# Differential attention in blocks of one query tile, with its value projection by head pair and its head norm taken in three batches

## The reference

```python
def diff_blocks(q, k, v, lam):
    scale = q.shape[-1] ** -0.5
    def blk(qb):
        s = jnp.einsum('bqhsd,bkhsd->bhsqk', qb, k).astype(jnp.float32) * scale
        p = jax.nn.softmax(s, axis=-1)
        a = (p[:, :, 0] - lam * p[:, :, 1]).astype(v.dtype)
        return jnp.einsum('bhqk,bkhd->bqhd', a, v)
    return over_query_blocks(blk, q)
...
    o_diff = diff_blocks(dq, k_d.reshape(b, -1, DIFF_HEADS, 2, DIFF_HD), v_d, lam)
    o_diff = (rmsnorm(o_diff, lp['diff_subln']) * (1.0 - lam_init)).reshape(b, n, GROUP_W)
```

## Time and profile before

| | |
|---|---|
| median of three runs | 2740.01 us (2735.83 to 2743.49) |
| the profiled execution, time | 2737.1 us |
| its span in the trace | 2734.9 us |
| mean granted PE clock | 0.942 |
| busy: PE, DVE, ACT, POOL | 2426.1, 1319.2, 943.0, 172.8 us |

### The profile page before, as it was taken

One profiled execution on the slowest core, in us unless ns is written; L12 is line 12 of the kernel. 1 busy time (PEld: TensorE's weight loads), 2 busy tenths in 40 slices (PEclk: granted clock), 3 DMA queues, 4 the chain that ended last, 5 costly groups with the idle time before them and its releaser, 6 DMA issues. The chain is left out here.

```text
span 2734.9 us, 33688 instructions
## 1 busy us (share of the span) xinstructions
PE 2426.1 (89%) x13152; PEld 1596.1 (58%) x13152; DVE 1319.2 (48%) x2658; ACT 943.0 (34%) x1886; POOL 172.8 (6%) x184
## 2 busy tenths in 40 slices
PE   3999999899898987879859999999988989888798
PEld 1765765674476756554327567557745667565543
DVE  3352664564364474661133426545553644746611
ACT  2242113541253364651022421135412533646510
POOL 0120000001000000001202200010010000000012
PEclk8999999999999998989969999999999989989799
DMA  6430100100100000102155101000001000001021
GB/s 216 165 140 26 50 16 1 48 1 13 58 7 9 3 1 2 63 1 91 60 178 213 61 26 50 16 21 29 1 13 64 1 9 3 1 2 63 1 93 61
DMA packets 72136, 128.42 MB, mean 47 GB/s; under 512 B 22915, under 2 KB 36099, under 8 KB 70341
## 3 DMA queue, kind: packets, MB, share of 16 engines
q1 hardware_dynamic: 71864, 121.52, 13.0%
q10 hardware_dynamic: 112, 4.72, 0.5%
HBM read 109.02 MB, written 21.92 MB: 48 GB/s over the span
## 5 line engine op out<-in xcount | busy, mean ns | idle before, releaser
L609 PE MATMUL psum<-arena 128*32 128x256 f32 (+8 forms) x8496 | 1743.0, 451 | 123.8 <-DMA arena<-in_hy_decay 46.9
L609 PEld LDWEIGHTS psum<-arena 128*32 128x32 f32 (+3 forms) x8496 | 1013.1, 161 | 780.7 <-issue 526.3
L613 PE MATMUL psum<-ident,arena 128*128 128x128 f32 (+1 forms) x2248 | 366.6, 291 | 76.2 <-ACT arena L1284 30.0
L1763 DVE TENSOR_REDUCE st<-psum 128x1 f32<-128x1152 f32 (+1 forms) x288 | 352.0, 1235 | 137.1 <-PE psum L609 135.5
L1469 DVE TENSOR_TENSOR arena<-arena 128x64 f32<-128x64 f32 (+10 forms) x686 | 304.5, 490 | 175.8 <-ACT arena L1420 57.5
L613 PEld LDWEIGHTS psum<-ident,arena 128*128 128x128 f32 (+1 forms) x2248 | 268.1, 146 | 178.6 <-issue 59.7
L1268 ACT ACTIVATE arena<-psum,st 128x1152 f32<-128x1152 f32 (+1 forms) x288 | 324.8, 1129 | 118.8 <-DVE st L1763 115.3
L609 PE MATMUL psum<-k_parts,q_parts 96*128 96x384 f32 (+2 forms) x1000 | 300.4, 391 | 34.4 <-ACT arena L1268 22.9
L1284 ACT COPY arena<-psum 128x512 f32<-128x512 f32 (+1 forms) x344 | 170.6, 505 | 230.3 <-PE psum L613 229.2
L1469 DVE TENSOR_TENSOR arena<-psum,arena 128x512 f32<-128x512 f32 (+2 forms) x136 | 75.1, 553 | 355.6 <-PE psum L609 308.2
L609 PEld LDWEIGHTS psum<-k_parts,q_parts 96*128 96x128 f32 (+1 forms) x1000 | 181.5, 205 | 53.3 <-ACT arena L1268 36.6
(11 more groups left out here) (125 smaller groups left out, 1170.1 us busy)
## 6 DMA issues: line engine op xcount, KB each, us to landing
arena<-in_ada_w SPq DMA_DIRECT2D x12, 2048.0 KB, 9.0
arena<-in_w_in SPq DMA_DIRECT2D x10, 2048.0 KB, 9.0
arena<-out_xs SPq DMA_DIRECT2D x36, 512.0 KB, 4.7
out_xs<-arena SPq DMA_DIRECT2D x18, 512.0 KB, 2.6
arena<-in_w_out SPq DMA_DIRECT2D x4, 2048.0 KB, 7.9
out_xs<-in_x ACTq DMA_DIRECT2D x1, 4608.0 KB, 17.3
spectrum_kept<-arena SPq DMA_DIRECT2D x2, 2304.0 KB, 8.4
arena<-spectrum_kept SPq DMA_DIRECT2D x2, 2304.0 KB, 8.8
```

The lines of the kernel that those rows point to most:

```text
L609: return nc.tensor.matmul(out, lhsT, rhs, start=start, stop=stop)
L613: return nc.tensor.transpose(out, src, ident[0:n, 0:n])
L1763: nc.vector.tensor_reduce(st[:, 16 + x % 4:17 + x % 4], psum[:, 512 * b0:512 * (b0 + nk)].rearrange("p (c n) -> p c n", c=nk)[:, :, 0:w], ...
```

## The change

Differential groups leave `attention` and get programs of their own on PE, ACT and DVE (`diff_attention`). A block becomes one query tile with both heads: nine blocks, and still 18 units and 24 steps. Value products come at every second step from step 4, 36 matmuls of 128 moving columns instead of 256. The output is not divided by the softmax sums: since the head norm divides by the root of the mean square, the sums cancel except in the small constant, which is multiplied by the squared sums instead (`squares`, and four extra matmuls in `head_squares`). So `inverse_sums`, `spread_sums`, `spread_out` and `finish` fall away, and DVE only copies the block out of bank 7 (`read_out`, 128 columns). The norm runs for three batches of blocks, 0 to 3, 4 to 7 and 8, at steps 10, 18 and 20. The value projection for the sample is made in each group for its own two heads, 128 columns wide, in steps 0 to 3 (`sample_values`), and read out in two copies of four tiles. All three gate parts are multiplied before the attention. Banks 6 and 7 alternate by another rule, and four probability buffers replace three. The rotary table (`ROPE_DIFF`) lies elsewhere and is loaded in each group. `VALUE_FILL` is the table of steps 0 to 3.

```diff
-BLOCKS = {g: [(tiles, p) for tiles in QUERY_TILES for p in range(len(PAIRS[g]))] for g in PAIRS}
+QUERY_TILES = {1: [(0, 1), (2, 3), (4, 5), (6, 7), (NT,)], 2: [(t,) for t in range(TT)]}
+BLOCKS = {g: [(tiles, p) for tiles in QUERY_TILES[MAPS[g]] for p in range(len(PAIRS[g]))] for g in PAIRS}
+HEADS_NORMED = ((0, 4), (4, 8), (8, 9))
...
-    if fills(grp, u + 2):
-        return 6
+        return (7, 6, 7)[j] if u % 2 else (6, 6, 7)[j]
...
+        return 2 * (n % 2) + i
...
-def fills(grp, g):
-
-    if grp == "diff0" and g < 5:
-        return [("v", t) for t in ((0, 1), (2, 3), (4, 5), (6,), (7,))[g]]
-    if grp == "diff0":
-        return {7: [("gate", 1, slice(0, 2))], 8: [("gate", 1, slice(2, 5))], 9: [("gate", 1, slice(5, KD))],
-                13: [("gate", 2, slice(0, KD))]}.get(g, [])
-    if grp == "diff1":
-        return {0: [("gate", 1, slice(0, 3))], 1: [("gate", 1, slice(3, 6))], 2: [("gate", 1, slice(6, KD))],
-                4: [("gate", 2, slice(0, KD))]}.get(g, [])
-    return []
+def normed(g):
+
+    return [b for b, (n0, n1) in enumerate(HEADS_NORMED) if g == 2 * (n1 - 1) + 4]
...
-                load(at(ROPE_DIFF, NT, 64), I["rope"][:, :, 0:64], "diff_params")
...
+                    load(at(ROPE_DIFF, NT, 64), I["rope"][:, :, 0:64], "diff_rope", part)
...
+                def sample_values(grp, half, first):
+
+                    job, c = ("v", grp, half), P * int(grp[4])
+                    ps = claim(job, [7]) if first == 0 else bank[7]
+                    for i in (first, first + 1):
+                        t = 4 * half + i
+                        for k in range(KD):
+                            last = mm(ps[:, i * P:(i + 1) * P], hT[:, k, t * P:(t + 1) * P],
+                                      W[:, SLOT["diff_vg", 0], k, c:c + P], k == 0, k == KD - 1)
+                    if first == 2:
+                        last.then_inc(*K.done(job))
...
+                def diff_attention(grp):
+
+
+                    units, steps = UNITS[grp], tail_step(grp)
...
+                    def scores(u, s):
+
+                        n, i, _ = units[u]
+                        t, x = BLOCKS[grp][n][0][0], 2 * u + s
+                        if x >= 2:
+                            pe.wait_ge(*S.at("exps", (grp, x - 2)))
+                        for j, (c, w) in enumerate(chunks(t)):
+                            last = mm(bank[3 * (x % 2) + j][:, 0:w], q_parts[0:96, 2 * i + s, t * P:(t + 1) * P],
+                                      k_parts[0:96, 2 * i + s, c:c + w])
+                        last.then_inc(*S.up("scores", (grp, x)))
+
+                    def turn(u, j):
+
+                        if not (0 <= u < len(units) and j < pieces(grp, u)):
+                            return
+                        number, b = piece_number(grp, u, j), turn_bank(grp, u, j)
+                        pe.wait_ge(*S.at("mixed", (grp, u)))
+                        kts = key_tiles(grp, units[u][0])[4 * j:4 * j + 4]
+                        take_bank(b, S.at("turned_scalar", (grp, number)))
+                        for a in range(len(kts)):
+                            last = flip(bank[b][:, a * P:(a + 1) * P], at(PROB[grp] + (u % 4) * 1152 + (4 * j + a) * P, P))
+                        last.then_inc(*S.up("turned", (grp, number)))
+
+                    def values(n):
+
+                        kts = key_tiles(grp, n)
+                        take_bank(7, S.at("read_out", (grp, n)))
+                        if n == 0:
+                            pe.wait_ge(*K.emptied(("v", "diff", NT)))
+                            pe.wait_ge(*K.emptied(("v", grp, 1)))
+                        pe.wait_ge(*S.at("turned_scalar", (grp, piece_number(grp, 2 * n + 1, pieces(grp, 2 * n + 1) - 1))))
+                        for kt in kts:
+                            for i in range(2):
+                                prob = at(SLOTS[grp], 4, TT, P)[:, slot(grp, 2 * n + i), kts.index(kt), :]
+                                for w in range(2):
+                                    row0, vc = 64 * i + 32 * w, P * int(grp[4]) + 64 * i + 32 * w
+                                    last = mm(bank[7][row0:row0 + 32, 0:P], at(VV + kt * GW + vc, 32), prob,
+                                              kt == kts[0], kt == kts[-1])
+                        last.then_inc(*S.up("values", (grp, n)))
+
+                    def head_squares(b):
+
+                        n0, n1 = HEADS_NORMED[b]
+                        pe.wait_ge(*S.at("head_squares", (grp, b)))
+                        take_bank(7, S.at("roots_begun", (grp, b)))
+                        mm(bank[7][:, 0:(n1 - n0) * P], halves[:, :], at(DQ, (n1 - n0) * P), True, False)
+                        for k in range(n1 - n0):
+                            last = mm(bank[7][:, k * P:(k + 1) * P], at(TH["diff"] + k * P, P), ident[:, :],
+                                      False, k == n1 - n0 - 1)
+                        last.then_inc(*S.up("squares_summed", (grp, b)))
+
...
+                    for g in range(steps):
+                        if g < len(units):
+                            scores(g, 0)
+                        if g % 2:
+                            turn(g - 3, 1)
+                        if g < len(units):
+                            scores(g, 1)
+                        if g in VALUE_FILL:
+                            half, first = VALUE_FILL[g]
+                            if first == 0:
+                                take_bank(7, K.emptied(("v", grp, half)))
+                            sample_values(grp, half, first)
+                        for b in normed(g - 1):
+                            head_squares(b)
+                        turn(g - 3, 2)
+                        if g % 2:
+                            turn(g - 2, 1)
+                        turn(g - 2, 0)
+                        for n in due(grp, g):
+                            values(n)
...
-                        gate("diff", "diff_vg", GW, int(grp[4]), 0, K.next())
+                        for i in range(3):
+                            gate("diff", "diff_vg", GW, int(grp[4]), i, K.next())
...
+                    def head_roots(b):
+
+                        nq = P * (HEADS_NORMED[b][1] - HEADS_NORMED[b][0])
+                        act.wait_ge(*S.at("squares_summed", (grp, b)))
+                        nc.scalar.activation(at(DQ, nq), bank[7][:, 0:nq], ACT.Ln, scale=1.0 / 64
+                                             ).then_inc(*S.up("roots_begun", (grp, b)))
+                        act.wait_ge(*S.at("roots_begun", (grp, b)))
+                        nc.scalar.activation(at(DQ, nq), at(DQ, nq), ACT.Exp, scale=-0.5).then_inc(*S.up("head_roots", (grp, b)))
+
+                    def keep_samples(half):
+
+                        job, c = ("v", grp, half), P * int(grp[4])
+                        act.wait_ge(*K.full(job))
+                        nc.scalar.copy(at(VV, NKEY, GW)[:, 4 * half:4 * half + 4, c:c + P],
+                                       B(job).rearrange("p (a n) -> p a n", a=4)).then_inc(*K.drained(job))
...
+                        take(g - 3, 0)
+                        take(g - 3, 1)
+                        if g % 2 == 0:
+                            take(g - 3, 2)
                         if g < len(units):
                             exps(g, 0)
...
+                        if g == 3:
+                            keep_samples(1)
+                        for b in normed(g - 1):
+                            head_roots(b)
+                        if g % 2:
+                            take(g - 3, 2)
+                        if g < len(units):
+                            exps(g, 1)
+                        if g == 1:
+                            keep_samples(0)
...
+                    def read_out(n):
+
+                        v.wait_ge(*S.at("values", (grp, n)))
+                        nc.vector.tensor_copy(at(DD + n % 4 * P, P), bank[7][:, 0:P]).then_inc(*S.up("read_out", (grp, n)))
+
+                    def squares(b):
+
+                        n0, n1 = HEADS_NORMED[b]
+                        nu, c, d = 2 * (n1 - n0), 24 + 2 * n0 % 16, at(DD, (n1 - n0) * P)
+                        s0 = st[:, c:c + nu].unsqueeze(2).to_broadcast([P, nu, 64])
+                        nc.vector.scalar_tensor_tensor(at(TH["diff"], nu, 64), s0, 64 * EPS, s0, ALU.mult, ALU.mult)
+                        v.wait_ge(*S.at("read_out", (grp, n1 - 1)))
+                        tt(at(DQ, (n1 - n0) * P), d, d, ALU.mult).then_inc(*S.up("head_squares", (grp, b)))
+
+                    def head_norm(b):
+
+                        n0, n1 = HEADS_NORMED[b]
+                        nq = (n1 - n0) * P
+                        out = oT[:, OUT_TILE[grp], n0 * P:n1 * P]
+                        v.wait_ge(*S.at("head_roots", (grp, b)))
+                        link(tt(at(DD, nq), at(DD, nq), at(DQ, nq), ALU.mult))
```

(22 more changed lines are left out.)

295 lines of the change are left out of this document (133 added, 162 removed).

## The result

The changed kernel takes 2667.93 us (median of four runs, 2663.98 to 2677.52) against 2740.6 for the kernel before in the same comparison: a ratio of 0.9742, with a 95% interval of 0.9710 to 0.9773. That is 72.7 us less. The forecast was 2671 us.

The account below looks back on a forecast made before the run. Waits between engines, plus PE's fill in diff0, were taken to bound the differential stages. Body 85.1, tail 17.1 and 8.3 ahead made 110.5 us a stage, 67.2 us gained in two layers: 2671 us, forecast 2655 to 2690, range 2640 to 2708.

Parts of the forecast that it names:

- The pair of units: Two steps of the new pipeline: DVE longest at 8.8 us, slacks 0 to 0.4; 9.4 us taken, against 12.2 before.
- The term for the clock: In the bodies: granted clock stays near 0.85, so a pair takes 9.4 us instead of 8.8.
- the rival with the high clock: Clock stays high and slacks hold: 8.8 us a pair, 15.5 for the tail, 2650 us; chance 0.17.
- The first four units: Start of a body, steps with value projection: 4.9 us of PE each, 22.8 us until the fifth unit's maxima.
- The norm: Blocks 0 to 3, in steps 10 to 12: 3.5 us once a stage, where 1.7 to 1.9 came per block.
- A body: First scores into the last mix: first units, six pairs, norm and ends sum to 85.1 us.
- The tail's sum: Stage end after the last large mix: 15.5 us at full clock, 17.1 with a tail's clock; values 2.0.
- What moves ahead: Before the first scores: two gate parts add 8.3 us per stage; rotary table load hidden, 3 us at most otherwise.
- the signs named ahead: Expected profile: maxima 9.0 to 9.8 us apart, bursts 2.0 to 2.3, bodies 82 to 88, tails 15.5 to 18, clock near 0.85.
- Narrow products bound by issue: Rival in 32 value bursts: 0.082 us a record, 5.9 instead of 2.0 us a burst, 2783 us; chance 0.05.
- The chain: Rival: the chain between engines binds the pairs, not DVE; 10.5 to 11 us a pair, 2702 us; chance 0.15.
- No change in the steps: Rival: the pair stays at 12.2 us, 67 us more over 24 pairs, 2738 us; chance 0.03.

Follow-up runs that it names:

- e13: The changed kernel with every block's value products done twice in place; 2727.04 us, ratio 0.9937.
- e6: The changed kernel with the rotary table of diff0 loaded first among that stage's transfers; 2665.85 us, ratio 0.9742.
- e4: The changed kernel without the small DVE product that multiplies the reciprocal by lambda and the first sum; 2664.57 us, ratio 0.9724.
- e10: The changed kernel with ACT instead of DVE copying a block's output out of bank 7, all but each batch's last block; 2664.61 us, ratio 0.9741.
- e11: The changed kernel with each block's output normed by itself instead of in batches, the norm's place kept; 2700.74 us, ratio 0.9849.
- e12: The changed kernel with each block normed by itself and the norm moved to its old place, ahead of the scores; 2717.83 us, ratio 0.9909.
- e7: The kernel before with all gate parts ahead and one-tile blocks in the differential groups, old order and norm; 2756.31 us, ratio 1.0060.
- e1: The changed kernel with value products over one key tile instead of nine; 2686.74 us, ratio 0.9803.

## Why the prediction was right

**The pair of units** was the main term. DVE was named as the longest at 8.8 us with a slack of 0 to 0.4, and I chose 9.4 for the clock. Measured: 8.89 us, without idle time on DVE. The hand-made schedule held to 0.1 us, and e13 showed its slack behind the values to be as small as worked out (10.7 us expected and measured).

**The term for the clock was mis-sized.** "PE has as much work per time in the new pairs as in diff1 before" was wrong. PE is busy for 69.5 of 81.7 us in diff1's body, 85%, before 73.9 of 98.6, 75%, and the clock there is 0.97, not 0.85. Of the bodies of layer 0, some 15 and 29 us were at 1.2 GHz before, and 4 and 4 are in the change. Six pairs at 0.5 less make 3.1 us a body. So the pairs went as the rival with the high clock has them, not as the forecast; its tail did not.

**The first four units** were put at 22.8 us behind 0.9 of scores; from the first scores (947.38) to the fifth unit's maxima (970.18) are 22.8 in all. Projection steps took 3.73 us (3.6 expected), and the wait of step 3 is the 3.11 in front of 970.18. **The norm** of blocks 0 to 3 was put at 3.5; the four units around it take 21.4 instead of 17.8 us, 3.7 more. **A body** came to 81.8 instead of 85.1.

**The tail's sum left out a burst.** It had one value burst behind the last large unit; there are two, since block 6 comes due in the step after that mix (1030.22, 3.01 us with half the clock). 17.1 + 3.0 is 20.1; measured 20.3 in diff0 and 21.2 in diff1. That both bursts lie on the tail's path shows in e13: with both doubled, diff0's tail takes 24.5 us, 4.3 more.

**What moves ahead** was put at 8.3. Diff1 shows 8.5 (58.8 us from the stage's start to the first scores, before 50.3). Diff0 shows 11.4: the rotary table was called hidden, argued from diff1 alone. In diff0 it is issued late among the loads and DVE waits for it, 1.4 us longer than before for its last load. The rest, 1.7 us, is by estimate what another 3.4 us at 1.2 GHz cost, since the granted clock was at half once in this stretch before and twice in the change. In e6 both are missing, and diff0 shows 8.1.

**The sum fitted by luck in part.** The body was put 3.3 and 3.5 us too long (diff0, diff1), the tail 3.2 and 4.1 too short, and these cancel. What is left is mostly diff0's 3.1 us ahead of its scores: the stages take 113.5 and 111.3 us where 110.5 was forecast for each. They gave 23.6 and 5.8 us in layer 0 of the profiled execution, 29.4 where 33.6 were forecast, and 32.5 in layer 1. The profiled execution itself took 9.6 us more than the median; diff0 starts 5.9 us later in it than before, in work that the change does not touch, with 62 instead of 48 us at 1.2 GHz up to there. By medians the gain is 72.7. So the gain read in the stages, 61.9 us, is below the forecast's 67.2, and that of the medians above it.

**Of the signs named ahead** the value bursts (2.17 us), the idle time before DVE's maxima in the pairs and, nearly, the projection records (3.73) came. The pairs (8.9, not 9.0 to 9.8), the bodies (81.6 to 82.1, not 82 to 88), the tails (over 18) and the clock (0.97, not near 0.85) fell outside or at the edge, and one of the signs of being wrong came: DVE waits for the rotary table in diff0.

**Narrow products bound by issue** (5.9 us a burst) did not come: 72 records in 2.17 us are 0.030 a record. The Trainium skill ("TensorE: Matmul & The Clock Gate", section "Back-to-back issue gap") gives some 81 ns for each matmul of a sustained stream with 128 columns. This trace does not agree for these narrow records: they take 30 ns each, four side by side 0.121 us. **The chain** did not bind beyond DVE, but e4 and e10 show it level with DVE, and e11 and e12 show how little it takes. **No change in the steps** came in e7, which has the narrow bursts without the rest.

## What to carry to other kernels

Where several engines pass one tile along, write two steps of all programs down with their durations: what stands ahead of the work that the longest engine waits for counts, and not only how long it is. e12 and e11 are the case: the same operations, with the norm ahead of the score maps or behind them, 11.4 or 10.6 us a pair at best. Where one of two like stages carries all of a piece of work, and the other has room for half of it, read both: 55.9 us for the first four units of both groups became 45.6 with the projection split. And a version with less work on one engine isn't a lower bound of the time: the clock may fall with it (e1).

## What the runs showed of the hardware

- Taking 64 of 72 value records out of each burst lowered the granted clock in a body from 0.98 to 0.80 and made the kernel 17 us slower (e1); doubling them gave 0.98 and 1.00 (e13).
- 72 f32 records with 32 weight columns and 128 moving columns take 2.17 us, 30 ns each; those with 128 weight columns take 3.73 us for 32, 117 ns each. So four narrow records, side by side, take 121 ns, about as long as one wide record.
